# A chained two-block transformer kernel: reordering its opening (loads, modulation, turned columns, first weight sums)

## The reference

```python
cond = jax.nn.silu(c)                               # 1024 values
mod = cond @ ada_w[i] + ada_b[i]                    # 3072 values
shift, scale, gate = jnp.split(mod[:, None, :], 3, axis=-1)
h = rms_norm_f32(x, norm_g[i]) * (1.0 + scale) + shift
proj = h @ w_in                                     # then q, k, v, g of the mixer
...
x = x + gate * out
```

## Time and profile before

| | before |
|---|---|
| median of 3 executions | 2437.29 us (2437.01 to 2437.52) |
| profiled execution | 2436.67 us |
| its span | 2434.8 us |
| busy TensorE / VectorE / ScalarE / GpSimd | 98% / 65% / 48% / 50% |

### The profile page before, as it was taken

One profiled execution on the slowest core, in us unless ns is written; L12 is line 12 of the kernel. 1 busy time (PEld: TensorE's weight loads), 2 busy tenths in 40 slices (PEclk: granted clock), 3 DMA queues, 4 the chain that ended last, 5 costly groups with the idle time before them and its releaser, 6 DMA issues.

```text
span 2434.8 us, 36011 instructions
## 1 busy us (share of the span) xinstructions
PE 2397.2 (98%) x13552; PEld 2050.1 (84%) x13552; DVE 1586.4 (65%) x2151; ACT 1172.9 (48%) x2308; POOL 1217.9 (50%) x883
## 2 busy tenths in 40 slices
PE   7999999999999999999999999999999999999999
PEld 6888898875578898899888888999988888888887
DVE  6976657588544286653666775777434489788864
ACT  5322223344444253322445555888534434888861
POOL 2645545431044455544555545666554546866664
PEclk9999999999999999999999999999999999999999
DMA  7554544484033344543333448655234253300034
GB/s 278 158 192 151 184 157 159 150 315 146 31 113 131 121 160 152 190 151 113 106 102 104 104 124 227 161 148 143 78 119 164 99 169 114 104 1 1 4 127 156
DMA packets 295724, 329.21 MB, mean 135 GB/s; under 512 B 88264, under 2 KB 226304, under 8 KB 293760
## 3 DMA queue, kind: packets, MB, share of 16 engines
q1 hardware_dynamic: 294080, 326.81, 41.7%
q10 hardware_dynamic: 1472, 0.10, 0.0%
HBM read 247.53 MB, written 79.33 MB: 134 GB/s over the span
## 4 chain that ended last, share of the span: by engine, by line
PE 83%; DVE 8%; ACT 3%; issue 3%; DMA 1%; POOL 1%; SPq 1%; DVEq 0%; ACTq 0%
PE ps L1238 22%; PE ps L1240 22%; PE ps L1239 22%; PE ps L1575 3%; PE ps L1746 2%; PE ps L1727 2%; PE ps L1490 2%; PE ps L1509 2%; PE ps L1503 1%; PE ps L1561 1%; DVE s_raw L2432 1%; PE ps L1258 1%; PE ps L1473 1%; SPq L1007 1%; PE ps L1446 1%
## 5 line engine op out<-in xcount | busy, mean ns | idle before, releaser
L1124 POOL TENSOR_TENSOR w_lo<-raw,w_hi 128x512 fp32r<-128x512 f32 (+1 forms) x450 | 649.1, 1451 | 793.2 <-ACT w_hi L1852 757.5
L1852 ACT ACTIVATE w_hi<-raw 128x512 fp32r<-128x512 f32 (+1 forms) x454 | 281.4, 628 | 775.2 <-PE ps L1240 620.2
L1238 PE MATMUL ps<-w_hi,s_hi 128*128 128x256 f32 (+2 forms) x832 | 262.8, 316 | 0.7 <-DVE u L2552 0.3
L1239 PE MATMUL ps<-w_lo,s_hi 128*128 128x256 f32 (+2 forms) x832 | 262.0, 315 | 0.0
L1240 PE MATMUL ps<-w_hi,s_lo 128*128 128x256 f32 (+2 forms) x832 | 262.0, 315 | 0.0
L1124 POOL TENSOR_TENSOR w_lo<-raw_wide,w_hi 128x512 fp32r<-128x512 f32 x112 | 157.1, 1412 | 149.6 <-ACT w_hi L1852 149.6
L2552 DVE TENSOR_TENSOR u<-u,ps 128x1024 f32<-128x1024 f32 (+1 forms) x96 | 116.3, 1212 | 145.3 <-PE ps L1240 141.9
L1238 PE MATMUL ps<-w_hi,a_hi 128*128 128x256 f32 (+2 forms) x624 | 197.0, 316 | 0.8 <-POOL w_lo L1124 0.8
L1239 PE MATMUL ps<-w_lo,a_hi 128*128 128x256 f32 (+2 forms) x624 | 196.6, 315 | 0.0
L1240 PE MATMUL ps<-w_hi,a_lo 128*128 128x256 f32 (+2 forms) x624 | 196.5, 315 | 0.0
L1238 PE MATMUL ps<-s_hi,w_hi 128*128 128x512 f32 x480 | 188.6, 393 | 3.1 <-DVE s_lo L2419 2.2
(11 more groups left out here) (349 smaller groups left out, 6239.7 us busy)
## 6 DMA issues: line engine op xcount, KB each, us to landing
raw<-in_w SPq DMA_DIRECT2D x158, 512.0 KB, 4.1
ada_c<-in_ada SPq DMA_DIRECT2D x14, 2304.0 KB, 10.8
blk<-u SPq DMA_DIRECT2D x46, 512.0 KB, 4.5
raw_wide<-in_w SPq DMA_DIRECT2D x32, 512.0 KB, 4.6
blk<-c SPq DMA_DIRECT2D x23, 512.0 KB, 3.5
blk<-m1s SPq DMA_DIRECT2D x23, 512.0 KB, 3.3
ada_first<-in_ada SPq DMA_DIRECT2D x12, 768.0 KB, 15.9
r_g<-blk SPq DMA_DIRECT2D x8, 1024.0 KB, 9.8
```

Of the source, the lines that this page charges most:

```text
L1124: pool.tensor_tensor(w_ring(w_lo, n), w_source(n), w_ring(w_hi, n).bitcast(F32), ALU.subtract)\
L1238: pe.matmul(out, a_hi_, b_hi_, start=first, stop=False, skip_group_check=True)
L1239: pe.matmul(out, a_hi_, b_lo_, start=False, stop=False, skip_group_check=True)
L1852: act.activation(w_ring(w_hi, n), w_source(n), ACT.Copy).then_inc(w_rounded, 1)
```

## The change

- **Loads.** SP issues pieces 2 and 0, R11, the first quarter for block 1, pieces 3 and 1, R21, the second quarter for block 1, the second half of x, R12, R22.
- **Modulation.** Pieces 2, 0 and 1 are summed by TensorE: nine matmuls each, with the condition repeated over 32 columns (`c_wide`) as the stationary operand and a slice of 512 columns moving. Slices go in turn to four groups of 32 output partitions. VectorE copies the bank to `acc_first`, and `first_columns` adds one partition of each group up into columns. Piece 3 is still summed by VectorE.
- **Columns in two parts.** Columns 0 to 3 (pieces 0 and 2) are made before (0,0); columns 4 to 7 (pieces 1 and 3) within (1,0). Only the first part is waited for before (0,0), and 20 transposes of the identity into an unused bank stand ahead of that wait.
- **x in two parts.** Tiles 4 and 5 of the first half are turned at the start of (1,0), tile 6 in it, tile 7 at the start of (0,1). The second half's tiles 4 to 7 are turned at the start of (1,1), its tiles 0 to 3 in the middle of (1,1). ScalarE's and VectorE's lists are reordered to match.
- **Weight sums.** The four sums of block 0 are made by GpSimd: 0 and 1 before its low halves for (1,1), 2 and 3 before those for (0,2). GpSimd's wait on `first_acc` is gone.

```diff
 x_first = place("x_first", 64, [P, 4, D])
-ada_first = [place(f"ada_first{n}", at, [P, ADA, 512]) for n, at in enumerate((0, 18, 36, 80))]
+ada_first = [place(f"ada_first{n}", at, [P, ADA, 512]) for n, at in enumerate((18, 80, 0, 40))]
+c_wide = place("c_wide", 98, [P, ADA + 1, 32])
 acc_first = place("acc_first", 100, [P, 4, 512])
...
 def turn_bank(l, a, k):
-    return k - 2 if (l, a) == (0, 0) and k >= 4 else 4 + k % 4
+    return 4 + k % 4
+def turn_columns(l, a, k):
+    return l + 2 if l or a or k >= 4 else 1
 TURNED_ACT, TURNED_DVE = ((0, 2, 4, 6), (4, 5, 6, 7, 0, 2, 3)), ((1, 3, 5, 7), (1,))
...
     x_load(0, 0, b)
-for n in (1, 0, 2, 3):
+def load_ada(n):
     for c in (2, 0, 1):
...
             .then_inc(ada_in[(0, None, 1, 2)[n]][c] if n != 1 else ada_second, 16)
+load_ada(2)
+load_ada(0)
 load_raw(R11, 0)
 load_second(0, 0)
+load_ada(3)
+load_ada(1)
 load_raw(R21, 0)
+load_second(0, 1)
 for b in range(4):
     sp.dma_start(x_first[:, b], t["x"][(4 + b) * P:(5 + b) * P, :]).then_inc(x1_got[b], 16)
-load_second(0, 1)
 load_raw(R12, 0)
...
         .then_inc(w_split, 1)
+def first_weight_sum(n):
+    dst, left, right = WEIGHT_SUMS[n]
+    if n:
+        pool.wait_ge(sums_done, n)
+    if n == 0:
+        pool.wait_ge(ld[R11], 16 * raw_load(R11, 0))
+        pool.wait_ge(ld[R12], 16 * raw_load(R12, 0))
+    if n == 1:
+        pool.wait_ge(ld[R22], 16 * raw_load(R22, 0))
+    if n == 2:
+        pool.wait_ge(w_split, product_end(0, 0))
+    if n == 3:
+        pool.wait_ge(w_split, product_end(0, 1))
+    pool.tensor_tensor(raw_quad(dst, 0), raw_quad(left, 0), raw_quad(right, 0), ALU.subtract)\
+        .then_inc(sums_done, 1)
 def queries(g):
...
 end = len(WSLOTS) if LAST == 2 else PRODUCT[FIRST_BLOCK[LAST + 1], 0]
-pool.wait_ge(first_acc, 3)
 for n in range(end):
+    if n == PRODUCT[1, 1]:
+        first_weight_sum(0)
+        first_weight_sum(1)
+    if n == PRODUCT[0, 2]:
+        first_weight_sum(2)
+        first_weight_sum(3)
     if LAST > 0 and n == OUT[1, 0]:
...
 for k in tiles:
-    if (l, a) == (0, 0):
-        if k >= 6:
-            turned_evac(pe, 0, 0, k - 6)
-    elif turn_place(a, k) >= 4:
+    if turn_place(a, k) >= 4:
         turned_evac(pe, l, a, (k + 4) % 8)
-    elif l == 0:
-        for n in (6, 7):
-            turned_evac(pe, 0, 0, n)
     elif a:
...
 if s - 1 in FIRST_BLOCK[0:3]:
-    if (s, i) == (1, 0):
-        for n in (4, 5):
-            turned_evac(pe, 0, 0, n)
     if i == 1:
...
         mm.then_inc(w_used, 1)
+def first_rows(bank, piece, slices):
+    for n in slices:
+        k, group = (6, 7, 8, 0, 1, 2, 3, 4, 5)[n], slice(32 * (n % 4), 32 * (n % 4) + 32)
+        mm = pe.matmul(ps[group, bank, :], c_wide[:, k], ada_first[piece][:, k], start=(n < 4),
+                       stop=(n >= 5), skip_group_check=True)
+        if n == ADA - 1:
+            mm.then_inc(cols_done, 1)
+def first_columns(bank, piece):
+    pe.wait_ge(first_acc, (2, 4, 1, 3)[piece])
+    over = ones[:, 0:1] if piece == 3 else c_wide[:, ADA, 0:1]
+    for j in range(4):
+        mm = pe.matmul(ps[:, bank, 4 * piece + j:4 * piece + j + 1], acc_first[:, piece, j * P:(j + 1) * P],
+                       over, start=True, stop=True, skip_group_check=True)
+    if piece < 2:
+        mm.then_inc(cols_done, 1)
 def block_product(l, s, i):
...
 added = i == 1 and s - 1 in FIRST_BLOCK[0:3]
+if (s, i) == (1, 0):
+    turn_half(0, 0, (4, 5))
+if (s, i) == (0, 1):
+    pe.wait_ge(cols_ready, 2)
+    turn_half(0, 0, (7,))
 bank_wait(s, i)
...
     pe.wait_ge(x_split, 1)
-if (s, i, k) == (FIRST_BLOCK[l] + 1, 0, 1 if l else 2):
+if (s, i, k) == (1, 0, 3):
+    turned_evac(pe, 0, 0, 3)
+    for piece in (3, 1):
+        first_columns(7, piece)
+    turn_half(0, 0, (6,))
+if (s, i, k) == (1, 0, 1):
+    turned_evac(pe, 0, 0, 2)
+    pe.wait_ge(ada_second, 16 * 3)
+    first_rows(6, 1, range(ADA))
+if (s, i, k) == ((FIRST_BLOCK[l] + 1, 0, 1) if l else (1, 1, 0)):
     turn_half(l, 1, range(4, 8))
-if (s, i, k) == ((FIRST_BLOCK[l] + 1, 0, 3) if l else (0, 1, 0)):
+if (s, i, k) == ((FIRST_BLOCK[l] + 1, 0, 3) if l else (1, 1, 2)):
     turn_half(l, 1, range(4))
...
     mm.then_inc(a_sdone, 1)
-pe.wait_ge(c_ready, 1)
-pe.wait_ge(dve_init, 2)
 pe.wait_ge(const_in, 16 * 3)
-pe.wait_ge(ada_second, 16 * 3)
-for j in range(4):
-    for k in range(ADA):
-        rhs = ccol[:, 0, k:k + 1] if k < KD else ones[:, 0:1]
-        pe.matmul(ps[:, 0, 4 + j:5 + j], ada_first[1][:, k, j * P:(j + 1) * P], rhs, start=(k == 0),
-                  stop=(k == KD), skip_group_check=True)
-turn_half(0, 0, range(6))
-for n, piece in enumerate((0, 2, 3)):
-    pe.wait_ge(first_acc, n + 1)
-    for j in range(4):
-        mm = pe.matmul(ps[:, 0, 4 * piece + j:4 * piece + j + 1], acc_first[:, piece, j * P:(j + 1) * P],
-                       ones[:, 0:1], start=True, stop=True, skip_group_check=True)
-mm.then_inc(cols_done, 1)
-turn_half(0, 0, range(6, 8))
+pe.wait_ge(dve_init, 9)
+for c in (2, 0, 1):
+    pe.wait_ge(ada_in[1][c], 16)
+    first_rows(0, 2, [3 * ((c + 1) % 3) + n for n in range(3)])
+pe.wait_ge(ada_in[0][2], 16)
+first_rows(1, 0, range(3))
+turn_half(0, 0, range(4))
+first_columns(2, 2)
+for c in (0, 1):
+    pe.wait_ge(ada_in[0][c], 16)
+    first_rows(1, 0, [3 * (c + 1) + n for n in range(3)])
+first_columns(2, 0)
+for n in range(20):
+    pe.transpose(ps[:, 3, (n % 4) * P:(n % 4 + 1) * P], ident[:, :], ident[:, :])
 pe.wait_ge(cols_ready, 1)
...
         act.wait_ge(n_turned, 8 * half_of(l, a))
-    act_link(act.activation(m1s[:, :] if l == 0 and a else xn[:, b], src[:, b], ACT.Square,
+    act_link(act.activation(c11[:, :] if l == 0 and a else xn[:, b], src[:, b], ACT.Square,
                             accum_out=n_st[:, 0, l, 4 * a + b:4 * a + b + 1]))
...
 def turned(l, a, k):
-    act.wait_ge(cols_ready, l + 1)
+    act.wait_ge(cols_ready, turn_columns(l, a, k))
     act.wait_ge(n_turned, 8 * half_of(l, a) + turn_place(a, k) + 1)
...
     hi(PRODUCT[s + 1, 0] + 1)
-m1s_copy(s)
-product_slots(s, 1)
+    m1s_copy(s)
+    product_slots(s, 1)
+else:
+    m1s_copy(s)
+    product_slots(s, 1)
+    for b in range(2):
+        stats(0, 1, b)
+    for c in range(2):
+        turned(0, 0, 4 + 2 * c)
+        variant(0, "a12", c)
+    for b in range(2, 4):
+        stats(0, 1, b)
+    product_slots(s + 1, 1)
+    m1s_copy(s + 1)
 for k in (4, 5):
...
     turned(l, 1, k)
-m1s_copy(s + 1)
-hi(PRODUCT[s + 1, 1])
+if l:
+    m1s_copy(s + 1)
+    hi(PRODUCT[s + 1, 1])
 variant(l, "a22", 1)
 turned(l, 1, 0)
-hi(PRODUCT[s + 1, 1] + 1)
+if l:
+    hi(PRODUCT[s + 1, 1] + 1)
 for k in (2, 3):
...
     hi(PRODUCT[1, 0] + j)
-for k in (4, 6):
-    turned(0, 0, k)
-for b in range(4):
-    stats(0, 1, b)
-for c in range(2):
-    variant(0, "a12", c)
 def r_tables(s, i):
...
 s = FIRST_BLOCK[l]
+for b in range(4 if l else 0):
+    normalized(l, 1, b)
 if l:
-    for b in range(4):
-        normalized(l, 1, b)
-for n in range(2 if l else 0, 3):
-    weight_sum(s, n)
+    weight_sum(s, 2)
 variant_low(l, "a22", 0)
 turned(l, 1, 1)
-weight_sum(s, 3)
+if l:
+    weight_sum(s, 3)
 variant_low(l, "a22", 1)
...
 dve.memset(ones[:, :], 1.0).then_inc(dve_init, 1)
-dve.wait_ge(dve_init, 2)
+dve.memset(c_wide[:, KD], 1.0).then_inc(dve_init, 1)
+dve.memset(c_wide[:, ADA], 0.0).then_inc(dve_init, 1)
+dve.wait_ge(dve_init, 4)
+for g in range(4):
+    dve.memset(c_wide[32 * g:32 * g + 1, ADA, 0:1], 1.0).then_inc(dve_init, 1)
+dve.wait_ge(const_in, 48)
+dve.wait_ge(c_ready, 1)
+dve.tensor_copy(c_wide[:, 0:KD], ccol[:, 0, 0:KD].unsqueeze(2).to_broadcast([P, KD, 32])).then_inc(dve_init, 1)
 for b in range(4):
     normalized(0, 0, b)
-dve.wait_ge(const_in, 48)
-dve.wait_ge(c_ready, 1)
-for n, piece in enumerate((0, 2, 3)):
-    total = acc_first[:, piece]
-    for k in (6, 7, 0, 1, 2, 3, 4, 5):
-        if k % 3 == 0:
-            dve.wait_ge(ada_in[n][k // 3], 16)
-        addend = ada_first[piece][:, KD] if k == 6 else total
-        ins = dve.scalar_tensor_tensor(total, ada_first[piece][:, k], ccol[:, 0, k:k + 1], addend, ALU.mult,
-                                       ALU.add)
-        if k == 5:
-            ins.then_inc(first_acc, 1)
-        else:
-            link(ins)
+def first_rows(n, bank, piece):
+    dve.wait_ge(cols_done, n)
+    dve.tensor_copy(acc_first[:, piece], ps[:, bank]).then_inc(first_acc, 1)
+def first_columns(n, half, bank):
+    dve.wait_ge(cols_done, n)
+    part, at = slice(4 * half, 4 * half + 4), 4 * half
+    dve.tensor_copy(cols[:, 0, 0, part], ps[:, bank, at:at + 4])
+    dve.scalar_tensor_tensor(cols[:, 0, 1, part], ps[:, bank, KD + at:KD + at + 4], 1.0, norm_col[:, 0, part],
+                             ALU.add, ALU.mult).then_inc(cols_ready, 1)
+    dve.wait_ge(cols_ready, half + 1)
+first_rows(1, 0, 2)
+first_rows(2, 1, 0)
 link(dve.tensor_scalar(gains[:, 0:1], gains[:, 0:1], gains[:, 1:2], -P ** -0.5, ALU.mult, ALU.mult))
-dve.wait_ge(cols_done, 1)
 dve.wait_ge(pos_in, 16)
-dve.tensor_copy(cols[:, 0, 0], ps[:, 0, 0:KD])
```

(30 more changed lines are left out.)

## The result

The changed kernel takes 2440.92 us, the median of 20 runs (2438.48 to 2442.8). The kernel before takes 2437.25 on the same chip (20 runs, 2435.92 to 2438.84). The ratio is 1.0015, with a 95% interval of 1.0009 to 1.0021: 3.67 us more, which is under the 0.2% that counts as a difference here; but the interval lies wholly above 1, so a small loss is real. The forecast was 2438.8 us and "same"; the profiled execution took 2440.95 us around a span of 2439.1.

What follows compares the result with a forecast made beforehand. TensorE's stream, 98% busy, bounds the kernel; the opening's 12.7 + 1.6 us go into 6.8 us of moved work and waits. S1's +1.65 less about 0.1 gives +1.5, so 2438.8 us; range 2433 to 2445.

Steps and rivals of the forecast that it cites:

- "same": Forecast verdict for the whole time: a difference under 0.2%, 4.9 us; chance 0.70.
- The opening: TensorE up to (0,0): first product at 27.5 us instead of 40.16, 12.7 us earlier; (0,0) ends at 33.0.
- Rivals B and C: Opening: B, clock stays low, 2444.6 us, 13%; C, column groups run one after another, 2447.8 us, 7%.
- The clock's 1.6 us: Product (0,0): 20 added transposes fill TensorE's wait and raise the granted clock, saving 1.6 us.
- Landings: Load arrival times from DMA rates: piece 1 at 35.0 us, R12 at 44.9; late by some us, 5%.
- S1: Start of s1's first half on VectorE: 65.35 us against 63.70 before, +1.65; the end moves with it.
- Rival A: Opening passes through to the end because VectorE, rid of its sums, no longer limits: -7.5 us, 2429.8; 10%.
- The clash: GpSimd's weight sums and VectorE's low halves and normalizations stretch each other; (1,1) starts at 57.4 us.
- the upper bound: GpSimd's sums beside VectorE before (1,1): a clash each time, so (1,1) starts at 59.3 us.
- "+1.5": Forecast change of the whole time: S1's +1.65 us less 0.1 or so given back, so 2438.8 us.

Runs made afterwards that it cites:

- e10: Changed kernel without the 20 identity transposes ahead of the first product; 2440.47 us.
- e3: Changed kernel with piece 1 loaded ahead of piece 3; 2440.41 us.
- e9: Changed kernel with the edits of e6, e7 and, with 16 transposes for 24, of e8; 2436.12 us.
- e1: Changed kernel with block 0's four weight sums back on VectorE in their old places, new opening kept; 2438.28 us.
- e4: Changed kernel with R12 and R22 loaded right after R21, ahead of the second half of x and (0,1)'s second quarter; 2436.71 us.
- e8: Changed kernel with 24 identity transposes in TensorE's wait ahead of (0,1); 2441.68 us.
- e2: Changed kernel with weight sums 1 to 3 only 8 columns wide instead of 256, sum 0 whole; 2438.17 us.
- e6: Changed kernel with e3 and e4 together, sums 0 and 1 ahead of (0,1)'s low halves on GpSimd, ScalarE's statistics spread out; 2436.95 us.
- e7: e4 with weight sums 2 and 3 on VectorE behind the last normalization; 2437.31 us.

## Why the forecast was right, point by point

**The opening: right.** First product 26.93 (forecast 27.5); nine slices over four column groups 2.73 us (3.0); norm_col there at 21.1, 19.0 us after its issue (22.5); (0,0) over at 32.65 (33.0). Rivals B and C are ruled out by these rows: the nine slices side by side took 2.73 us, the sixteen transposes at 17.78 took 1.97, and the narrow matmuls had been slow only up to 13.6. The clock's 1.6 us were sized nearly rightly, as e10 shows by losing 1.45 in (0,0); they were worth nothing, since the next wait, for piece 1, ends at the same time either way.

**Landings: 0.9 to 1.7 us late.** Piece 1 landed at 36.74 (35.0), R12 when GpSimd began at 46.29 (landing at 44.9, sum 0 from 45.4). TensorE stood before (0,1) at 46.6 instead of 45.55. That the time of piece 1 passes through to S1 is shown by e3.

**The opening doesn't pass through: right.** Rival A needed (1,1) before 50.9 with the sums off VectorE; it starts at 59.45, and in none of the changed kernel's variants before 53.80 (e9). With the sums back on VectorE the time is that of before, within the measurement (e1).

**The clash: right in kind, too small.** This is the mis-sized term. The forecast gave bounds of 53.3 and 59.3 us for (1,1)'s start and took 57.4; measured 59.45. Each of the five 128x1024 operations from 47.37 on, all reading SBUF, was caught, by 1.1, 2.0, 1.1, 0.8 and 1.9 us, which is the case that the upper bound described. Counted from the start of sum 0, (1,1) came after 13.2 us; the forecast had 12.0 and its upper bound 13.9. So of the 2.05 us by which (1,1) was later than forecast, 0.9 are the late landing and 1.2 the clash. From there to S1 7.58 us were needed (7.95), which makes 67.03 (65.35), at the top of the 64 to 67 given. The prediction's own list for the clash could have said so: it is written out step by step, each step a full clash, and nothing in the rows spoke for fewer. The trace shows how large one can be: a normalization of 0.75 us took up to 2.71 beside GpSimd's sums, of which one alone takes 2.43 (e4).

**Where "+1.5" became +3.67.** S1 is 1.7 later than forecast and 3.3 later than before; near 400 us it is 3.2. The last 0.4 is within the scatter. The loss was forecast at less than half its size; "same" held because both sizes lie under 0.2%. e1 and e4 show the cause from both sides: with the sums away from GpSimd 3.0 of the 3.2 us are gone, and with the sums on GpSimd but earlier, 4.2. With only piece 1 earlier 2.4 are gone (e3). These don't add up, because each changes the same thing, whether the sums and VectorE's work for (0,1) and (1,1) fall together. What the late piece would cost with no clash at all was not tried.

**What was left out.** The low clock in (0,1)'s second half (0.50 from 56 to 58 us) was not foreseen. It lies on the chain of waits, but e8 shows that (1,1) starts no sooner without it. In e1, e2 and e6 it does count: there (1,1) follows (0,1)'s slow matmuls without a wait for VectorE.

**What stays open.** e3, e6, e7 and e9 keep their earlier start near 400 us and at 1484 us, but their medians are 1.6 to 2.4 us above what that would give. Behind 400 us the profiles differ most just after 1484 us, where attention starts and TensorE waits for a_pT: from GpSimd's first a_p to its first write of the tile a_bias 22.3 us pass in before, 22.4 in e4, 23.1 in e9, 23.2 in e7, 24.6 in e6 and 24.8 in e3. So e3's and e6's loss lies there; of e7's and e9's their profiles show 0.8 to 0.9. The windows of e3 and under it of e4:

```profile
1485.00:1505.00 20.00, 14.38 (x94) 13.38 (x95) 9.18 (x37) 10.75 (x28) 8.50 (x9) 0.83 0.89 243
```

```profile
1485.00:1505.00 20.00, 15.69 (x125) 14.74 (x122) 10.60 (x40) 13.53 (x35) 7.98 (x9) 1.00 0.85 229
```

From 1484 us to the end the four profiles with a clock of 0.83 there take 952.4 to 953.8 us, the seven with 0.91 take 950.4 to 952.3, and e4, with 1.00, 950.5. What decides which of them an execution gets was not tried.
